# The block compression of a hybrid decoder step on TensorE: from 128-row transposes and plain float32 products to 64-row halves and split float32 products

## What is computed

```python
q, kv_c, kv_s, kv_w, gates, u = split_proj(rms_norm(x, g_attn) @ w_in)     # "projection"

def compress_blocks(kv, pe, w1, w2):                  # blocks of 64 tokens, 2 groups g, keys/values c
    blocks = kv.reshape(B, L // 64, 64, 2, 2, 64) + pe[:, None]
    hid = jax.nn.gelu(jnp.einsum('bnlgcd,cldh->bngch', blocks, w1))   # sum over l (64) and d (64), h = 128
    return jnp.einsum('bngch,chd->bngcd', hid, w2)

past_c = cache_cmp[page_table]                        # 8 sequences, 32 blocks each, 16.8 MB in float32
comp = concat([compress_blocks(past_c), compress_blocks(new rows)])
# then: attention over comp, top-16 blocks selected from cache_slc, window attention over state_win,
# pooling heads, output projection, MLP with 4096 hidden columns
```

## Time and profile before

| | us |
|---|---|
| three runs | 950.17, 952.62, 955.35 |
| median | 952.62 |
| the profiled execution | 951.2 |
| its span, first to last instruction | 949.4 |
| PE busy | 872.4 (92%) |
| DVE busy | 440.8 (46%) |
| ACT busy | 335.1 (35%) |
| POOL busy | 120.3 (13%) |
| mean granted clock of TensorE | 0.957 |

### The profile page before, as it was taken

The page is one execution under the profiler, slowest core; times in us unless marked ns, Lnnn a source line. Parts: engine busy times, 40 slices in busy tenths (PEclk is TensorE's granted clock), DMA queues, the critical chain, the costliest instruction groups (busy, mean ns, idle before and its releaser), DMA issues.

```text
span 949.4 us, 15754 instructions
## 1 busy us (share of the span) xinstructions
PE 872.4 (92%) x6263; PEld 766.6 (81%) x6263; DVE 440.8 (46%) x969; ACT 335.1 (35%) x594; POOL 120.3 (13%) x119
## 2 busy tenths in 40 slices
PE   5999969998689877899799999999999999999994
PEld 4999946665455454656699999999999999999994
DVE  5426435444566757556523743234333343334324
ACT  7501034444245556545423432123311341123202
POOL 0000001330433442552022000000000000000000
PEclk8999979999698997999899999999999999999997
DMA  8923046782500001542622222112222222222002
GB/s 279 350 74 117 12 135 222 279 292 91 221 2 0 0 13 66 208 166 91 181 89 89 90 89 70 58 55 83 88 88 88 88 88 88 88 88 88 0 0 100
DMA packets 48769, 102.51 MB, mean 108 GB/s; under 512 B 7498, under 2 KB 19166, under 8 KB 46429
## 3 DMA queue, kind: packets, MB, share of 16 engines
q1 hardware_dynamic: 41821, 68.47, 21.3%
q0 software_dynamic: 6912, 33.56, 9.4%
HBM read 97.61 MB, written 8.53 MB: 112 GB/s over the span
## 4 chain that ended last, share of the span: by engine, by line
PE 49%; DVE 1%; ACT 1%; issue 0%; DVEq 0%; ACTq 0%
PE bank L1916 49%; DVE low L1903 1%; ACT low L1829 0%; DVE wl L1842 0%; PE bank L1958 0%; ACT wh L1785 0%; ACT small L1835 0%; DVE small L1900 0%; DVE hT L1880 0%; DVE hT L1855 0%; DVE xl L1859 0%; ACT low L1799 0%; DVE xl L1848 0%; ACT xh L1801 0%; DVEq L1740 0%
## 5 line engine op out<-in xcount | busy, mean ns | idle before, releaser
L1916 PE MATMUL bank<-xh,wh 128*128 128x288 f32 x640 | 137.9, 297 | 4.3 <-DVE xl L1848 3.9
L1916 PE MATMUL bank<-xl,wh 128*128 128x288 f32 x640 | 137.5, 297 | 0.0
L1916 PE MATMUL bank<-xh,wl 128*128 128x288 f32 x640 | 137.5, 297 | 0.0
L1785 ACT ACTIVATE wh<-low 128x1024 fp32r<-128x1024 f32 x72 | 75.2, 1052 | 121.3 <-PE bank L1916 121.0
L1916 PE MATMUL bank<-ah,wh 128*128 128x288 f32 x512 | 109.7, 296 | 0.0
L1916 PE MATMUL bank<-al,wh 128*128 128x288 f32 x512 | 109.6, 296 | 0.0
L1916 PE MATMUL bank<-ah,wl 128*128 128x288 f32 x512 | 109.6, 296 | 0.0
L1916 PEld LDWEIGHTS bank<-xh,wh 128*128 128x128 f32 x640 | 103.8, 190 | 4.9 <-DVE wl L1842 4.1
L1916 PEld LDWEIGHTS bank<-xh,wl 128*128 128x128 f32 x640 | 103.7, 190 | 0.0
L1916 PEld LDWEIGHTS bank<-xl,wh 128*128 128x128 f32 x640 | 103.7, 190 | 0.0
L1880 DVE TENSOR_TENSOR hT<-bank,hT 128x288 f32<-128x288 f32 x64 | 26.3, 452 | 139.0 <-PE bank L1916 139.0
(11 more groups left out here) (313 smaller groups left out, 1316.6 us busy)
## 6 DMA issues: line engine op xcount, KB each, us to landing
low<-in_w_up SPq DMA_DIRECT2D x8, 2048.0 KB, 8.9
low<-in_w_down SPq DMA_DIRECT2D x8, 2048.0 KB, 7.8
zone<-in_cmp_w SPq DMA_DIRECT2D x16, 256.0 KB, 8.4
o_swin<-in_state_win SPq DMA_DIRECT2D x8, 504.0 KB
px<-in_x_prompt SPq DMA_DIRECT2D x4, 512.0 KB, 5.0
u_raw<-in_w_in SPq DMA_DIRECT2D x1, 2048.0 KB, 9.9
q_raw<-in_w_in SPq DMA_DIRECT2D x1, 2048.0 KB, 10.2
low<-in_state_win SPq DMA_DIRECT2D x4, 512.0 KB
```

The costliest lines, as they stand in the source:

```text
L1785: act.activation(wcols(m.wh, i), raw_cols(i), ACT.Copy).then_inc(wh_ready, 1)
L1916: last = pe.matmul(out(i, hf), w[wi], half(x[:, k, :], hf), start=first and part == 0, stop=end and part == 2)
```

## The change

- **One block.** `project` and `compress` no longer open a block of their own. Each returns five functions, and `build` makes one block in which each engine runs the list of `project` and then that of `compress`. The barrier is replaced by waits on the projection's own semaphores. SP's wait for all written states stands at the very end of the program. `w1` of chunk 0 and the second chunk of the cache are loaded during the projection.
- **Transposes as halves.** A unit is two positions. `turn(u)` makes 16 transposes of 64 rows instead of 8 of 128 rows: rows 0 to 63 go to one bank, rows 64 to 127 to another.
- **fp32r products.** ACT copies each bank, all 128 rows, to `blkh` in fp32r, DVE makes `blkl` of the rest. `w1` is split into `w1h` and `w1l`, once a chunk. Keys and values lie on rows 0 to 63 and 64 to 127, so each product is 64 rows deep. A unit has 12 products of 512 columns, in turn for keys and values, into banks 0 and 1.
- **The prompt in 64x32 tiles.** The prompt's blocks and the position code are 17 columns of `blkp`, used as weights; `w1` moves (128 columns), in plain float32. There are 16 such products a chunk, on eight tiles of 64 rows by 32 columns. The position code is one of the 17 columns and comes back as a bias after the loop.
- **Moved transfers.** The page transfers of the first pair and its windows are issued in `prompt`, since the memory that they fill now holds `blkh` and `blkl`.
- The loop is written out, 32 units, without a hardware loop.

```diff
-            with act.Fori(0, CHUNKS // 2) as it:
-                for v in range(2 * CHUNK_L):
-                    lo = HD * (v % 2)
-                    act.wait_ge(blk_turned, it * (2 * CHUNK_L) + v + 1)
-                    act.activation(m.blkT[(v // 2) % 2][0][lo:lo + HD, :], pb[4 + v % 4][0:HD, :], ACT.Identity,
-                                   bias=m.peT[0:HD, bass.ds(it * (2 * CHUNK_L) + v, 1)]).then_inc(blk_kept[0], 1)
+        for u in range(UNITS):
+            if u % CU == 2 and u // CU + 1 < CHUNKS:
+                split_w1(u // CU + 1)
+            act.wait_ge(blk_turned, u + 1)
+            if u >= RING:
+                act.wait_ge(hid_done, u - RING + 1)
+            for r in range(2):
+                act.activation(m.blkh[u % RING][:, r, :], pb[4 + 2 * (u % 2) + r][:, :], ACT.Copy).then_inc(blk_hi, 1)
...
+            for r in range(2):
+                dve.wait_ge(blk_hi, 2 * u + r + 1)
+                dve.tensor_tensor(m.blkl[u % RING][:, r, :], pb[4 + 2 * (u % 2) + r][:, :],
+                                  m.blkh[u % RING][:, r, :].bitcast(F32), ALU.subtract).then_inc(blk_lo, 1)
...
-                    for hg in range(4):
-                        a = KV * l + P * (hg % 2)
-                        last = pe.transpose(pb[4 + v % 4][:, P * hg:P * hg + P], m.raw[s][:, hg // 2, a:a + P], ident)
-                    last.then_inc(blk_turned, 1)
+        def turn(u):
+            ck = u // CU
+            if u % CU == 0:
+                pe.wait_ge(sems.raw_in[ck % 2], 32 * (ck // 2) + 32)
+            if u >= 2:
+                pe.wait_ge(blk_lo, 2 * u - 2)
...
+            for q in range(2):
+                for hg in range(4):
+                    at = KV * (2 * (u % CU) + q) + P * (hg % 2)
+                    for r in range(2):
+                        half = slice(64 * r, 64 * r + 64)
+                        to = 256 * q + 64 * hg
+                        last = pe.transpose(pb[4 + 2 * (u % 2) + r][:, to:to + 64],
+                                            m.raw[ck % 2][half, hg // 2, at:at + P], ident[half, half])
+            last.then_inc(blk_turned, 1)
+        def hidden(u):
...
+            pe.wait_ge(blk_lo, 2 * u + 2)
+            for q in range(2):
+                a = 2 * (u % CU) + q
+                for part in range(3):
+                    for c in range(2):
+                        w = (m.w1h, m.w1l, m.w1h)[part][ck % 2][half[c], a, :]
+                        x = (m.blkh, m.blkh, m.blkl)[part][u % RING][half[c], :, 256 * q:256 * q + 256]
+                        last = pe.matmul(pb[c][:, :], w, x, start=u == 0 and q == 0 and part == 0,
+                                         stop=u == UNITS - 1 and q == 1 and part == 2)
+            last.then_inc(hid_done, 1)
+        def hidden_prompt(ck):
+            for a in range(CHUNK_L):
+                l, j = CHUNK_L * ck + a, a % 4
                 for c in range(2):
+                    half = slice(HD * c, HD * c + HD)
+                    last = pe.matmul(pb[2 + c][32 * j:32 * j + 17, 0:P], m.blkp[half, l, :],
+                                     m.w1[ck % 2][half, a, :], start=False, stop=False, skip_group_check=True,
+                                     tile_position=(HD * c, 32 * j))
...
+        for u in range(UNITS + 1):
+            if u < UNITS:
+                turn(u)
+            if u:
+                if (u - 1) % CU == SMALL_AT:
+                    hidden_prompt((u - 1) // CU)
+                hidden(u - 1)
...
 def on_sync(sp):                                  # compress
+        sp.wait_ge(sems.unit_mm, 5)
+        load_w1(sp, m, sems, 1)
+        for ck in range(2, CHUNKS):
+            sp.wait_ge(w1l_ready, ck - 1)
+            sp.wait_ge(hid_done, CU * (ck - 2) + SMALL_AT + 1)
+            load_w1(sp, m, sems, ck)
...
@@ prompt, gpsimd
             pool.memset(m.kc2, 0.0).then_inc(sems.cleared, 1)
-            for x in range(4):
-                for e in range(2):
-                    load_pages(pool, m, 1, e, x, sems)
+            for n in range(2):
+                for x in range(4):
+                    for e in range(2):
+                        load_pages(pool, m, n, e, x, sems)
```

More of the change, by code:

```diff
@@ L57 @@
 CHUNKS = BLK // CHUNK_L
-LP = CHUNK_L // 2
+RING = 4
 CHUNKF = CHUNK_L * KV
@@ new lines, in on_sync, with on_gpsimd @@
+        sp.wait_ge(ut_kept, 3)
+        for b in range(NB_SEQ):
+            a = USAM * (b % 4) + DEC
+            sp.dma_start(m.o_spool[0, b], m.utok[a:a + HIST, b // 4, :]).then_inc(states_out, 16)
+        sp.dma_start(m.o_ppool[0, 0], m.utok[0:HIST, 2, :]).then_inc(states_out, 16)
+    def on_gpsimd(pool):
+        pool.memset(m.zeros[:, :], 0.0).then_inc(sems.cleared, 1)
+        pool.memset(m.ones[:, :], 1.0).then_inc(sems.cleared, 1)
+        pool.wait_ge(rows_mm, 2 * TILES)
+        pool.memset(m.uT[:, :, 0:HIST], 0.0).then_inc(upad, 1)
+        pool.wait_ge(idx_step, 7)
+        pool.wait_ge(wl_ready, UNIT0 + 4)
+        pool.wait_ge(sp_step, SP_TURNED)
+        load_chunk(pool, m, sems, 0)
@@ new lines, in compress, with on_sync, on_gpsimd @@
+    SMALL_AT = 1
+    UNITS = BLK // 2
+    CU = CHUNK_L // 2
+    def on_sync(sp):
+        sp.dma_start(m.pe_in[0:BLK, :], m.cmp_pe[0].rearrange("l c d -> l (c d)")).then_inc(pe_step, 16)
+        sp.wait_ge(sems.unit_mm, 5)
[4 more added lines that the diff above has]
+            load_w1(sp, m, sems, ck)
+    def on_gpsimd(pool):
+        for ck in range(1, CHUNKS):
+            if ck == 1:
+                pool.wait_ge(sems.wl_ready, 12)
+                pool.wait_ge(sems.unit_mm, 5)
+            else:
+                pool.wait_ge(blk_turned, CU * (ck - 1))
+            load_chunk(pool, m, sems, ck)
@@ L1003, in prompt @@
+    return on_sync, on_gpsimd, on_scalar, on_vector, on_tensor
 def prompt(nc, m, sems, sem):
@@ L1034, in _ @@
         def _(sp):
-            for b in range(2, 4):
+            for b in range(4):
                 load_window(sp, m, b, b, sems)
@@ L1988, in build, with _ @@
         m.imp_g = m.spX[:, 0:96]
-        project(nc, m, sems, sem)
-        compress(nc, m, sems, sem)
+        sems.w1_in = [sem("w1_in0"), sem("w1_in1")]
+        stages = project(nc, m, sems, sem), compress(nc, m, sems, sem)
+        with nc.Block() as block:
+            @block.sync
+            def _(sp):
+                for engines in stages:
+                    engines[0](sp)
+            @block.gpsimd
+            def _(pool):
+                for engines in stages:
+                    engines[1](pool)
+            @block.scalar
+            def _(act):
+                for engines in stages:
+                    engines[2](act)
+            @block.vector
+            def _(dve):
+                for engines in stages:
+                    engines[3](dve)
+            @block.tensor
+            def _(pe):
+                for engines in stages:
+                    engines[4](pe)
         prompt(nc, m, sems, sem)
```

1090 lines of the change are left out of this document (541 added, 549 removed).

## The result

| | before | after |
|---|---|---|
| median of four runs, us | 953.75 | 939.49 |
| lowest and highest, us | 950.17, 955.35 | 936.51, 943.26 |
| the profiled execution, us | 951.2 | 936.5 |
| its span, us | 949.4 | 934.7 |
| mean granted clock | 0.957 | 0.949 |

The ratio is 0.987, 95% interval 0.983 to 0.991. The kernel is 1.3% faster, by about 14 us; the forecast was 934, with 926 to 943 for its own case. For the profiled pair the gain is 14.7 us, forecast was 17.4.

The account below looks back on a forecast made before the run. PE was taken to bound the compression loop. From 951.2, less 22.8 for the loop, plus 0.2 for copies and 5.2 for pages, gave 933.8, so 934 us; own range 926 to 943, wider range 919 to 954.

Parts of the forecast that it names:

- PE sets the end of the loop; halves run two by two: Compression loop: PE is the bound; products and transposes of two halves overlap, 1.4 us products and 0.5 us transposes a unit.
- Rival C: Compression loop: halves don't overlap, step 4.7 us, loop ends at 276, total 998 us; chance 0.07.
- rival A: Compression loop: weight loads or instruction issue bound it, 3.1 us a unit, total 947.7 us; chance 0.10.
- Start of the loop: Border of projection and compression: `hidden(0)` starts at 127.6, where PE started it at 135.95.
- The step, 2.65: Compression loop: 2.1 plus 0.1 for DVE's split and 0.4 for the prompt's products gives 2.6; 2.65 us taken.
- the low bound: Prompt's products in the loop: all eight tiles working at once, 0.4 us a chunk; lowest step 2.25 us.
- rival B: Compression loop: `w1` comes late and ACT blocks; at worst step 3.1 us, total about 947 us; chance 0.07.
- D, better than that: Prompt's tiles all work at once and pages cost 3: step 2.3, loop end 200.3, total 921 us; chance 0.11.
- The way from `turn` to the products: Compression loop: from the end of `turn` over the ACT and DVE copies to its products, 2.35 us.
- The pages: Start of the prompt: 16 issues on POOL instead of 8, first scaling 7.3 late; loss 5.2 us, between 3 and 8.
- a little more is made good: Prompt: part of the pages' delay is recovered, since scores and exponentials for four units are ready by then.
- At nothing: Everything else counted as no cost, such as SP's 40 writes of state; GELU stays, its four copies +0.2 us.

Follow-up runs that it names:

- experiment 5: Changed kernel with projection and compression as two blocks with a barrier between them again: 942.09 us, ratio 0.990.
- experiment 6: Two blocks with a barrier again, on the version of experiment 2 with early `w1`: 931.17 us, ratio 0.976.
- experiment 2: Changed kernel with the prompt's products one unit earlier, so that `w1` is requested one unit earlier: 925.06 us, ratio 0.972.
- experiment 3: Changed kernel with the three products of the keys' half together, then the three of the values' half, instead of in turn: 939.48 us, ratio 0.990.
- experiment 4: Version of experiment 2 with eight full transposes of 128 rows a unit, products still halves: 940.15 us, ratio 0.989.
- experiment 8: Version of experiment 2 with eight page transfers ahead of the first scaling, eight behind every other scaling: 920.38 us, ratio 0.969.
- experiment 9: Version of experiment 8 plus unused filler products, 40 behind the compression's last unit and 12 before the prompt's first transposes: 915.81 us, ratio 0.963.
- experiment 10: Version of experiment 2, all 16 pages ahead of the scaling, with the filler products of experiment 9: 923.97 us, ratio 0.969.

## Why the prediction was right, by its steps

The total was near, but partly by luck: two errors in the step of the loop cancelled. The other terms have to be judged each by itself.

- **PE sets the end of the loop; halves run two by two.** Right, for fp32r and for transposes, which no row of before had shown. Pairs of 512 columns are 0.23 apart (forecast 0.23), twelve products 1.27 from first to last start and 1.50 to what follows (forecast 1.4), 16 transposes 0.43 (0.5). Rival C is out. Of rival A nothing is seen: the 64-row loads do not add up to 0.11 each. The Trainium skill ("TensorE: Matmul & The Clock Gate", section "LDWEIGHTS (loading the stationary operand)") has the cost of a load by its columns alone; at 107 ns each, one after the other, the 28 loads of a unit would take 3.0 us by an estimate from that page, and whole steps of 1.95 with all of them were measured. Nor does it come out with two halves loading at once: by the same estimate, eight pairs of loads would take 0.86 us, and the sixteen transposes take 0.43.
- **Start of the loop.** `hidden(0)` forecast at 127.6, measured 127.63. Experiments 5 and 6 give one block 3.4 (partly at half clock) and 1.9 of these 8.3 us; the rest must be DVE's eight additions gone and `turn` ahead of the splits, which no run changed alone.
- **The step, 2.65.** The mean was 2.65, the end of the loop 211.2 to 211.4 (forecast 211.2), but two terms were wrong against each other. The prompt's 32 instructions take 0.38 from first to last start, about 0.7 of PE's time with both changes of shape. Once in four steps, and with PE's slack taken off, they add 0.11 a unit (experiment 2: four steps of 8.78 with them, two pairs of plain ones 8.34), where I took 0.4: all eight tiles at work, the low bound. And the term for `w1` was missing: in the earlier trace rows I read that it comes 9.0 us after the request in time, with 8.4 typical, and gave rival B 0.07. It was partly true, and its sign was there: ACT's idle time before the split ended on a transfer, five times, 9.0 us in all. The longest wait brought 6.8 us at half the clock with it; 3.4 more lie at the start of the loop and are not of `w1`. In experiment 2 the step is 2.30, and from its first product to its last the loop is 10.7 us shorter, some 9 of them by `w1` in time. So "D, better than that" was there, with B on top.
- **The way from `turn` to the products.** 2.23 to 2.33, forecast 2.35. Right.
- **The pages.** The first scaling came 7.2 late (forecast 7.3) and the first transposes 5.6 (7.3 less the 1.6 absorbed: 5.7). What failed is the step after it, "a little more is made good": nothing was. The third transposes were 7.6 late (31.4 us behind the first scores, 23.8 before), and so was the end, 7.7 for 5.2. Before, PE's clock was at half for 13.7 us of this stretch, now for 23.9. Most of the two us more lie there: from the first values products to the scores behind the second transposes it was 2.05 us (264.52 to 266.57), and now, at half clock, 3.56 (248.56 to 252.12). It was not tested by itself, since with filler and 16 issues the clock fell again.
- **At nothing.** GELU, states, position code: the first scores came 22.1 earlier, forecast 22.6 (22.8 less the 0.2). Right.

The sum 933.8 for 936.5 in the profiled run is off by the 2.5 of the pages, and little else. That the total was near does not make the step right: a kernel that lost some 9 us to late weights looked just as forecast.

## What to carry to other kernels

Where PE is bound by transposes and products of 64 useful rows, put all of it on row halves, transposes too, and compare the plain float32 form before a split is built: it may come within half a per cent. When a stage gets a fifth faster or more, list each load that it asks for by an event of its own and compare landing time with the new distance; move the request first. When issues of transfers move on an engine, ask whose first result they stand ahead of, and put there only as many as fit in its idle time.

## What the runs showed of the hardware

- PE starts a product of one row half beside one of the other that stands three places earlier in the program (experiment 3): pairs 0.23 us apart, in either order.
- 32 products of 64x32 tiles (eight tiles, 128 columns, plain float32) take 0.38 us from first to last start, and make a step 2.66 long instead of 1.95 to 2.21, with the changes of shape around them (experiment 2).
- A 64-row transpose of 64 columns costs 0.029 us in a stream of 16 on two halves (0.43 from the first start to the last), a full one of 128 rows 0.12 (0.82 for eight, experiment 4), and going from 64-row products to 128-row transposes 0.1 on top, and back 0.1 again.
- After a pause of PE of 4.0 to 4.8 us, the clock was at half: 0.43 for a pair instead of 0.23, 4.01 us instead of 2.20 for the 36 products behind the loop. Shorter pauses went either way: behind 2.77 us at the border the clock fell (changed kernel), and behind the same 2.19 us it stayed high in experiments 2, 6 and 8 and fell in 9 and 10.
